# Expert stage of a decoder layer: the big expert's activation transposes move behind the small expert's first unit

## The reference

```python
def expert_block(args):
    tok, wts, e = args
    xb = h_pad[tok]
    gu = xb @ w1[e] + b1[e]
    gate, up = gu[:, :D_EXPERT], gu[:, D_EXPERT:]
    gate = jnp.minimum(gate, SWIGLU_LIMIT)
    up = jnp.clip(up, -SWIGLU_LIMIT, SWIGLU_LIMIT)
    act = (up + 1.0) * (gate * jax.nn.sigmoid(SWIGLU_ALPHA * gate))
    yb = act @ w2[e] + b2[e]
    return yb * wts[:, None].astype(yb.dtype)
```

## Time and profile before

| what | value |
|---|---|
| median of 3 runs | 1885.47 us (1885.14 to 1885.61) |
| profiled execution, its own time | 1884.88 us |
| span of the profiled execution, first to last instruction | 1882.7 us |
| PE busy | 1833.5 us (97%) |
| PE weight loads busy | 1297.8 us (69%) |
| DVE busy | 1125.7 us (60%) |
| ACT busy | 943.4 us (50%) |
| POOL busy | 357.9 us (19%) |
| DMA, mean over the span | 276 GB/s |

### The profile page before, as it was taken

One profiled execution on the slowest core, in us unless ns is written; L12 is line 12 of the kernel. 1 busy time (PEld: TensorE's weight loads), 2 busy tenths in 40 slices (PEclk: granted clock), 3 DMA queues, 4 the chain that ended last, 5 costly groups with the idle time before them and its releaser, 6 DMA issues.

```text
span 1882.7 us, 27246 instructions
## 1 busy us (share of the span) xinstructions
PE 1833.5 (97%) x8597; PEld 1297.8 (69%) x8597; DVE 1125.7 (60%) x1363; ACT 943.4 (50%) x1312; POOL 357.9 (19%) x401
## 2 busy tenths in 40 slices
PE   8999999999999999997999999999999999999998
PEld 5888887887888888886655665566556655665563
DVE  6768767867867333446754655465545554565456
ACT  4766676676666222325543454345434553455441
POOL 0332332332330000013111212021202121112010
PEclk9999999999999999998999999999999999999999
DMA  5232232232241222456999999999999999999998
GB/s 194 93 120 86 89 120 92 83 131 92 84 134 65 90 101 93 160 204 272 396 421 421 422 421 422 422 422 421 421 422 422 421 421 422 422 421 421 421 420 347
DMA packets 95230, 520.07 MB, mean 276 GB/s; under 512 B 13364, under 2 KB 20700, under 8 KB 44888
## 3 DMA queue, kind: packets, MB, share of 16 engines
q1 hardware_dynamic: 87528, 501.08, 66.5%
q0 software_dynamic: 6944, 16.36, 2.3%
q10 hardware_dynamic: 720, 2.16, 0.3%
HBM read 511.52 MB, written 25.51 MB: 285 GB/s over the span
## 4 chain that ended last, share of the span: by engine, by line
PE 77%; DMA 12%; DVE 6%; issue 3%; ACT 2%; SPq 0%; DVEq 0%; ACTq 0%; POOL 0%; POOLq 0%
PE bank L1832 19%; PE bank L1256 15%; PE bank L1637 10%; DMA big<-in_w 9%; PE bank L1286 7%; PE bank L1852 7%; PE bank L1861 6%; DVE w_lo L2392 2%; PE bank L1331 2%; PE bank L1844 1%; PE bank L1314 1%; PE bank L1782 1%; PE bank L1398 1%; DVE x_lo L2404 1%; ACT w_hi L2097 1%
## 5 line engine op out<-in xcount | busy, mean ns | idle before, releaser
L2392 DVE TENSOR_TENSOR w_lo<-big,w_hi 128x2048 fp32r<-128x2048 f32 x141 | 321.9, 2291 | 209.4 <-ACT w_hi L2097 209.4
L2097 ACT ACTIVATE w_hi<-big 128x2048 fp32r<-128x2048 f32 x141 | 268.8, 1918 | 231.5 <-DMA big<-in_w 206.2
L1852 PE MATMUL bank<-big,keep 128*64 128x512 f32 x896 | 203.1, 598 | 0.0
L1256 PE MATMUL bank<-h_hi,wm_hi 128*128 128x512 f32 x416 | 172.1, 414 | 0.0
L2392 DVE TENSOR_TENSOR w_lo<-keep,w_hi 128x2048 fp32r<-128x2048 f32 x48 | 109.9, 2292 | 102.3 <-ACT w_hi L2097 102.3
L1256 PE MATMUL bank<-h_hi,wm_lo 128*128 128x512 f32 x416 | 162.6, 391 | 0.0
L1256 PE MATMUL bank<-h_lo,wm_hi 128*128 128x512 f32 x416 | 162.2, 390 | 0.0
L1832 PE MATMUL bank<-w_hi,x_hi 128*128 128x512 f32 x512 | 143.8, 403 | 4.3 <-DVE w_lo L2392 4.3
L2097 ACT ACTIVATE w_hi<-keep 128x2048 fp32r<-128x2048 f32 x48 | 92.2, 1921 | 105.4 <-DMA keep<-in_w 95.3
L1852 PEld LDWEIGHTS bank<-big,keep 128*64 128x64 f32 x896 | 60.0, 136 | 117.8 <-issue 117.8
L1832 PE MATMUL bank<-w_lo,x_hi 128*128 128x512 f32 x512 | 137.5, 390 | 0.0
(11 more groups left out here) (364 smaller groups left out, 3565.2 us busy)
## 6 DMA issues: line engine op xcount, KB each, us to landing
big<-in_w SPq DMA_DIRECT2D x290, 1024.0 KB, 12.4
keep<-in_w SPq DMA_DIRECT2D x94, 1024.0 KB
big<-in_w_mix SPq DMA_DIRECT2D x72, 512.0 KB, 3.3
keep<-in_w_tail SPq DMA_DIRECT2D x44, 512.0 KB, 3.3
keep<-in_x SPq DMA_DIRECT2D x8, 512.0 KB, 5.0
aux<-acum_rows SPq DMA_DIRECT2D x16, 256.0 KB, 4.0
big<-acum_rows SPq DMA_DIRECT2D x16, 256.0 KB, 3.5
keep<-y_tok SPq DMA_DIRECT2D x4, 1024.0 KB
```

The costliest lines, as they stand in the source:

```text
L1256: ins = pe.matmul(to[:], w[:, k], h[:, k], start=(k == 0 and w is hi and h is h_hi), stop=(k == KT - 1 and w is lo))
L1852: ins = pe.matmul(bank[2 * (c // 2)][r, :], x_s[:, n % 4, CS * (n // 4):CS * (n // 4 + 1)], raw[s][:, c * 512:(c + 1) * 512], start=False, ...
L2097: act.activation(w_hi[:, s], raw[r], ACT.Copy).then_inc(hi_ready, 1)
L2392: dve.tensor_tensor(w_lo[:, s], raw[r], w_hi[:, s].bitcast(F32), ALU.subtract).then_inc(lo_ready, 1)
```

## The change

The transposes of the big expert's activation leave the end of `step_b` (and the place before the loop) and stand in `step_s`, behind its first unit, which is a small one. `bias1_s`, which no longer stands behind them, gets two waits of its own, since it overwrites banks 0 and 2: for ACT's silu of bank 0 and DVE's clip of bank 2. On ACT the copy of the small expert's result, `take_y_s(j - 1)`, stands ahead of `take_act_b(j)`. No instruction of an engine's arithmetic is added or removed.

```diff
@@ def bias1_s(b):
                     pe.wait_ge(xsm_ready.sem, xsm_ready.at(b, 1))
                     pe.wait_ge(picks_ready.sem, picks_ready.at(b, 1))
+                    pe.wait_ge(sl_ready.sem, sl_ready.at(b, 1))
+                    pe.wait_ge(u_ready.sem, u_ready.at(b, 1))
                     for c in range(2):
@@ PE, def step_s(j, more):
                         unit(j, "S", p)
+                        if p == 0:
+                            turn_act_b(j, True)
                     turn_act_s(j, more)
@@ PE, def step_b(j):
                         unit(j, "B", p)
-                    turn_act_b(j + 1, True)
@@ PE, ahead of the loop
                 turn_x_s(0)
-                turn_act_b(0, True)
                 pairs(pe, body, False, False)
@@ ACT, def step_s(j, more):
-                    take_act_b(j)
                     if not isinstance(j, int) or j > 0:
                         take_y_s(j - 1)
+                    take_act_b(j)
```

## The result

| kernel | median us (range) | profiled execution | its span |
|---|---|---|---|
| before | 1885.16 (1883.74 to 1888.54, 20 runs) | 1884.88 | 1882.7 |
| after | 1889.19 (1887.28 to 1893.24, 20 runs) | 1890.79 | 1888.7 |

The ratio is 1.0022 with an interval of 1.0016 to 1.0029: 4.0 us slower. The forecast was 1884.9, with a range of 1883.0 to 1887.8; the result lies outside it.

A forecast was written before the change was run, and what follows sets the result against it. Bound: a DMA queue full from some point on. Steady run 1.4 us earlier, but lateness 2.1 - 2.7 = -0.6 us decides; middle and last pairs 0: 1884.88 - 0.6 = 1884.3, as median 1884.9, range 1883.0 to 1887.8.

The forecast's parts named there:

- The bound, and the middle pairs: Middle pairs: a full DMA queue sets the pace at 62.54 us; the change costs 0, within 0.2 us a pair.
- ACT's cover: Middle pairs: ACT's later high part still ends 0 to 0.2 us before the first `w2` split's DMA wait ends.
- ACT's first `w2` split still ended by its DMA: Sign for a middle pair: ACT's split of the first `w2` unit still waits for its DMA, today until 1265.82.
- The gain of the first pair: First pair: small bias and first slot's load come 1.42 us earlier, so the DMA's steady run starts about 1.4 us earlier.
- it had to queue behind the first, so it follows closely: First pair: the second load, issued only 0.3 us earlier, still follows the first load closely.
- The lateness on DVE and PE: First pair: transposes and DVE's low part 2.1 us late, so PE waits about 2.1 us, plus 0.3.
- the rival: First pair: clock falls behind PE's new wait, 1.7 us more, 3.8 us late; end +1.1 us, 1886.6; chance 0.25.
- The queue: Load issued at 942.7: landing 7.4 less 4.7 leaves 2.7 us of queue, so 2.1 us of lateness gives -0.6 us.
- a DMA share below 1 behind 950 us: Sign that the prediction is wrong: the DMA engines' busy share falls below 1 behind 950 us.
- The rule of the Trainium skill weighed ahead: LDWEIGHTS share, 34.78 of 60 us, gives PE two fifths spare; first pair's delay made good, -1.4 us; full gain's chance 0.10.
- The spare that it gives PE: Early pairs take 60.26 us against 62.54 in the middle, so PE has 2.3 us a pair to spare.
- The last pair and the end: Last pair: PE waits 1.0 us at most, hidden by DVE's 4.62 us wait for result rows; cost 0, at most 1.0.

The follow-up runs named there:

- e2: Kernel after, but the first pair keeps its transposes ahead of the small bias (PE's first pair written out): ratio 0.9995, end +0.13 us.
- e3: Kernel after with DVE's `last_places` moved behind its second `w2` low part of the first pair: ratio 0.9998, end -0.78 us.
- e1: Kernel before with the change made in the first pair alone (PE's first pair written out): ratio 1.0017, end +4.77 us.
- e5: Kernel before with one extra 2.29 us subtraction on DVE ahead of its first `w2` low part in the first pair: ratio 1.0023, end +4.74 us.
- e10: e3 with the first small input's copy ahead of the silu on ACT: ratio 1.0012, end +1.98 us.
- e9: Kernel before with nine unused products ahead of the fifth pair's second `w2` unit, PE's first five pairs written out: ratio 1.0010, end +0.41 us.
- e12: Kernel before with PE's first five pairs written out and no products added: ratio 1.0009, end +0.30 us.
- e8: Kernel before with four unused products ahead of the first pair's second `w2` unit (PE's first pair written out): ratio 1.0011, end +2.48 us.
- e7: Kernel before with nine unused products ahead of the first pair's second `w2` unit (PE's first pair written out): ratio 1.0021, end +2.88 us.
- e6: Kernel after with nine unused products filling PE's wait ahead of the first pair's second `w2` unit: ratio 1.0014, end +3.09 us.

## Why the prediction was wrong, step by step

**The bound, and the middle pairs: right.** The period is 62.48 us for 62.54, the DMA share 1.01 and the rate 422 GB/s. The forecast of 0 with bounds of 0.2 us a pair is what e2 shows over fourteen pairs (end +0.13). ACT's cover was put at 0 to 0.2 us and turned out to be nothing. The sign "ACT's first `w2` split still ended by its DMA" thus failed, but PE doesn't feel it: the low part is ready 0.7 us ahead of its product (1275.37 and 1276.09).

**The gain of the first pair: right in place, smaller in worth.** Forecast was an issue 1.42 us earlier; from t0 it is 6.0 - 4.8 = 1.2. The second load, forecast 0.3 us earlier, is not (7.8 us after t0 against 7.7). The step "it had to queue behind the first, so it follows closely" failed here: with nothing else in the queue the first load alone doesn't fill the 3 us between the two issues. The start is thus worth 0.4 us of bytes and not 1.4. e3, where this is all that is left, has 0.4 in the bytes and 0.78 at the end.

**The lateness on DVE and PE: right.** Transposes 2.37 us late (forecast 2.1), low part 2.26 (2.1), PE's wait 2.29 ("2 us or more").

**The clock: the rival came, and its size was right.** I gave the fall 0.25. It came in after, e1 and e5 alike, behind waits of 2.29 to 2.43 us, and in e10 behind one of 2.60: every wait of 2.29 us or more in these traces has it. The forecast's sum left its 1.57 us out, and the rival's had it: 2.1 + 1.7 = 3.8 us were worked out, 3.83 were measured. That the row near the end decides it would be hindsight, though. The same wait of 1.76 us stands there in all fourteen traces. In five of them (before, after, e2, e9, e12) the clock falls behind it and the 32 small matmuls take 8.78 or 8.79 us, and in the nine others it stays and they take 7.09, as here in e3:

```profile
1855.69 0.47 PE L1822 MATMUL bank<-bias_hl,pick_s 128*128 128x512 f32 x1 [1.76 <-ACT keep L2143]
1856.09 7.09 PE L1863 MATMUL bank<-big,keep 128*64 128x512 f32 x32
```

Middle pairs have both as well: waits of 1.90 and 1.87 us in before and of 2.07 in e8 leave the clock at 1.00, waits of 1.84 (e7, e8) and 1.96 (e12) don't. So in these traces a wait between 1.76 and 2.07 us may or may not bring the fall, and its length alone doesn't tell.

**The queue: the step that failed.** "It has 7.4 - 4.7 = 2.7 us of queue" treats the difference of two landing times as slack that can be used up free of charge to the last. By it the forecast turned 2.1 us of lateness into -0.6 us, and the rival turned 3.8 us into +1.1; the measured end is +4.39. The loads of L1530 behind the gap, counted in order of issue, in before and after (issue from t0 + landing time = landed):

```
load   before               after                landed later by
 1      6.0 +  4.7 = 10.7    4.8 +  4.6 =  9.4   -1.3
 2      7.7 +  5.8 = 13.5    7.8 +  4.8 = 12.6   -0.9
 9     23.1 +  9.0 = 32.1   27.0 +  4.8 = 31.8   -0.3
12     25.9 + 14.8 = 40.7   29.7 + 11.5 = 41.2   +0.5
17     45.7 +  7.5 = 53.2   49.5 +  5.6 = 55.1   +1.9
20     53.2 +  7.4 = 60.6   57.1 +  5.8 = 62.9   +2.3
```

The forecast looked at the shortest landings only. At the ninth load, with 9.0 us in before, it would have allowed a lateness of 4.3 us; the load is 3.9 late, and the queue is dry already (235 GB/s at 918 us). At the seventeenth it allows 2.8, and 3.8 late should cost 1.0; the load lands 1.9 late, though its 5.6 us say that something is still ahead of it. At the twentieth the cost has grown by another 0.4, with 5.8 us. So the rate is lost while landings are still above 4.7 us, as e8 shows too (339 GB/s at a share of 0.92). The prediction's own sign, a DMA share below 1 behind 950 us, came up in after as 0.98 and 0.99 between 957 and 963 us. It shows little of the loss: the rate there is 341 and 265 GB/s. The runs give the price in before's own order: 0.73 us late costs 2.5 us at the end of the trace, and 1.87 late costs 2.9. The slack of the first pair is not 2.7 us, but none.

**What made it good again: nothing.** The rule of the Trainium skill weighed ahead (Trainium Kernel Development and Optimization, section Performance Expectations) is to judge how far a kernel is from the chip's limits by the share of LDWEIGHTS (and by the arithmetic done), and not by that of the matmuls. Read as PE's spare, two fifths, it would have PE regain the 2.1 us within the first pair. It doesn't: +3.83 us at the first x48 is +4.20 at the second. The early pairs' period of 60.26 us was the better measure. The spare that it gives PE, 2.3 us a pair, is against the DMA's pace: PE uses it in the middle (1.1 to 1.3 us regained behind a fall of the clock), but not in the first pairs, where PE itself sets the pace.

**The last pair and the end: right.** DVE's wait for the result rows is 4.58 us. The wait of up to 1.0 us that was allowed for PE did not come; in the last step it has only the 1.76 us that it had before.

## What to carry to other kernels

Where a kernel goes from one bound to another (here from a filling ring to a full queue), the few microseconds at the changeover are carried to the end at full price or more, while 1.1 to 1.3 us of delay in the fourth or fifth pair are regained; so a change that is harmless in the steady loop is to be judged by its first iteration, with everything that stands in order on every engine behind what was moved. The difference between two landing times is not slack; sum the bytes over consecutive stretches instead, and look for the first one in which the rate falls. And an ordering change that makes PE wait longer than it did is to be priced twice, once for the wait and once for a possible fall of the clock behind it (here at 2.29 us and above every time, from 1.76 to 2.07 sometimes); a few products without use in the wait give the second part back (e6: 1.3 to 1.6 us).

## What was not expected of the hardware

- **The start of the stage moves.** t0 lies between 887.9 and 893.2 us in the traces of this case, with the same work ahead. Without taking it off, 1.4 of the 6.0 us between the two profiled spans would have been put down to the change.
- **With a longer program on PE the end takes longer.** With five pairs written out (e12, e9) DVE's last addition is +0.3 and +0.4 us from t0, but from there to the span's end it is 4.2 and 4.3 us where all the others have 2.8 to 3.1; the medians are 1.3 and 2.1 us above before. The rows of DVE's last addition and of the last store, of before and then of e9:

```profile
1873.54 6.26 DVE L2456 TENSOR_TENSOR keep<-bank,keep 128x512 f32<-128x512 f32 x8
...
1879.03 1.13 SPq L1621 DMA_DIRECT2D out_rows<-keep  x2
```

```profile
1873.42 6.26 DVE L2463 TENSOR_TENSOR keep<-bank,keep 128x512 f32<-128x512 f32 x8
...
1878.92 1.13 SPq L1622 DMA_DIRECT2D out_rows<-keep  x2
```

  The addition and the issue stand where they stood (to 0.1 us); what is longer comes after the issue: the last stores of 256 KB take 3.5 us to land in e9 and 3.4 in e12, and 2.4 to 2.6 in the twelve other traces. That the written-out loop is the cause is likely from these two, and by what way is open. It also means that e9's ratio, 1.0010, is not the price of its nine products; e12, the control, has 1.0009.
- **Share and rate part.** The DMA engines counted as 0.92 to 0.99 busy at 339 to 396 GB/s (e8) and as 0.99 at 265 (after), where a full queue gives 421 at 1.04. Counted from 1.00, the share would have shown 0.3 us lost in e8's two rows, and the rate shows 0.8.
- **The same wait, with and without a fall of the clock.** The wait of 1.76 us near the end has the same length and the same work around it in all fourteen traces, and the clock falls behind it in five. Such falls in the fourth and fifth pair (e7, e8, e12) put PE back by 1.1 to 1.3 us for a pair.
